# Latent attention in one TensorE kernel: value products in three rounded passes, two query tiles at a time

## The reference, cut to what matters

```python
def attend(q, k, v):
    s = jnp.einsum('bqhd,bkhd->bhqk', q, k).astype(jnp.float32) * (1.0 / math.sqrt(q.shape[-1]))
    p = jax.nn.softmax(s, axis=-1)
    return jnp.einsum('bhqk,bkhe->bqhe', p.astype(v.dtype), v)

def blocked_attention(q, k, v):          # q swept over 128-query blocks
    qb = q.reshape(B, L // Q_BLOCK, Q_BLOCK, H, d).swapaxes(0, 1)
    out = lax.map(lambda qi: attend(qi, k, v), qb)

y_mla = blocked_attention(q_m, jnp.concatenate([k_mc, k_m], axis=1), jnp.concatenate([mvc, mv], axis=1))
```

## Time and profile before

| | |
|---|---|
| median of 3 runs | 2731.52 us (2730.34 to 2733.38) |
| the profiled execution: its own time, its span | 2732.97 us, 2731.2 us |
| PE busy, share of the span | 2622.6 us, 96% |
| DVE busy, ACT busy, POOL busy | 1453.3 us, 1060.7 us, 484.9 us |
| mean granted clock of PE | 0.992 |
| the phase `mla`, first score to last value product | 481.7 to 684.1 us |

### The profile page before, as it was taken

The page is one execution under the profiler, slowest core; times in us unless marked ns, Lnnn a source line. Parts: engine busy times, 40 slices in busy tenths (PEclk is TensorE's granted clock), DMA queues, the critical chain, the costliest instruction groups (busy, mean ns, idle before and its releaser), DMA issues. The chain is left out here.

```text
span 2731.2 us, 36346 instructions
## 1 busy us (share of the span) xinstructions
PE 2622.6 (96%) x14641; PEld 2274.8 (83%) x14641; DVE 1453.3 (53%) x2039; ACT 1060.7 (39%) x1788; POOL 484.9 (18%) x323
## 2 busy tenths in 40 slices
PE   6999979999999999999999999999999999999999
PEld 2777777999777888888888999879989998878977
DVE  5745572433457666666658625447743524427751
ACT  3411543444245334334235224157732223237740
POOL 0001221332000000000000011048820002009930
PEclk9999999999999999999999999999999999999999
DMA  6543101000211121121121225332122113243222
GB/s 240 174 142 102 55 8 53 15 1 1 108 42 60 33 60 60 33 62 57 37 62 50 101 51 117 79 81 48 44 110 90 60 43 86 59 109 84 47 88 82
DMA packets 69683, 193.68 MB, mean 71 GB/s; under 512 B 8080, under 2 KB 26896, under 8 KB 68624
## 3 DMA queue, kind: packets, MB, share of 16 engines
q1 hardware_dynamic: 69520, 191.41, 23.2%
HBM read 148.88 MB, written 19.07 MB: 61 GB/s over the span
## 5 line engine op out<-in xcount | busy, mean ns | idle before, releaser
L2679 DVE SCALAR_TENSOR_TENSOR res<-ps,gates,res 128x1024 f32<-128x1024 f32 x120 | 148.6, 1279 | 100.0 <-PE ps L2804 100.0
L1319 PE MATMUL ps<-h_hi,pf_wh 128*128 128x346 f32 (+2 forms) x800 | 184.4, 334 | 0.2
L2538 ACT ACTIVATE wo_wh<-ff_raw 128x512 fp32r<-128x512 f32 x120 | 75.3, 628 | 278.7 <-DVE ff_raw L2649 114.2
L1319 PE MATMUL ps<-h_lo,pf_wh 128*128 128x346 f32 (+2 forms) x800 | 182.9, 332 | 0.0
L1948 DVE TENSOR_REDUCE da_negmax<-ps 128x1 f32<-128x1040 f32 x136 | 167.6, 1236 | 18.9 <-PE ps L1798 11.5
L1933 POOL TENSOR_TENSOR da_E<-da_E,da_F 128x1040 f32<-128x1040 f32 x68 | 164.7, 2422 | 5.7
L2804 PE MATMUL ps<-ff_h_hi,wo_wh 128*128 128x512 f32 x512 | 157.8, 389 | 1.4 <-DVE res L2679 1.3
L1841 PE MATMUL ps<-da_aT,v 128*128 128x128 f32 (+1 forms) x1224 | 157.5, 274 | 0.7 <-ACT qk L1905 0.7
L2804 PE MATMUL ps<-ff_h_lo,wo_wh 128*128 128x512 f32 x512 | 157.7, 389 | 0.0
L2804 PE MATMUL ps<-ff_h_hi,wo_wl 128*128 128x512 f32 x512 | 157.6, 389 | 0.0
L909 POOL MEMSET h_hi<- 128x112 f32 x2 | 0.4, 194 | 870.9 <-POOLq L66 870.9
(11 more groups left out here) (546 smaller groups left out, 6208.7 us busy)
## 6 DMA issues: line engine op xcount, KB each, us to landing
ff_raw<-w_ff SPq DMA_DIRECT2D x48, 512.0 KB, 3.5
ada_w<-w_ada SPq DMA_DIRECT2D x16, 1024.0 KB, 7.6
ff_raw<-w_in SPq DMA_DIRECT2D x20, 512.0 KB, 3.8
pf_raw<-w_in SPq DMA_DIRECT2D x20, 512.0 KB, 4.0
wo_raw<-w_out SPq DMA_DIRECT2D x18, 512.0 KB, 4.9
residual_spill<-res SPq DMA_DIRECT2D x16, 520.0 KB, 3.0
st_q<-st_q_rounded SPq DMA_DIRECT2D x32, 260.0 KB, 5.4
ada_w<-w_ada SPq DMA_DIRECT2D x4, 2048.0 KB, 17.0
```

Source lines behind the costliest of these rows:

```text
L1319: pe.matmul(bank(i * 2 + s, s)[c], wh[:, s, q * P:(q + 1) * P], x(q)[:, a:a + ln], start=(q == 0 and n == 0), stop=False)
L2538: act.activation(ring(wh, i), src, ACT.Copy).then_inc(s_hi, 1)
L2679: last = dve.scalar_tensor_tensor(out=res[:, m, :], in0=k.ps[:, b:b + 2, :].rearrange("p c w -> p (c w)"), scalar=gate[:, m:m + 1], in1=re ...
```

## The change

The value product is made in three rounded passes, and for two query tiles together.

- `mv` writes the values as `vh` (ACT) and `vl` (DVE).
- The turned E goes to `aT_hi` and `aT_lo`, each with room for the two tiles of a pair side by side (256 columns per key tile). There is one such pair of buffers, not two.
- ACT rounds batches 0 and 2 (`round_turned`). DVE makes both parts of batch 1 and the rests of batches 0 and 2 (`rest_turned`); the rest of batch 2 stands behind the reciprocal, the others ahead of it.
- `pv` runs only in turns with odd i, and does 30 float32r products of 256 columns. It waits for the rests of batches 0 and 1, and from key tile 8 on for that of batch 2.
- PE may write bank 6 again when DVE's rest is done (`s_lo`) and not when ACT's copy is; `out` copies 256 columns once per pair.

```diff
@@ turn (PE)
                         if g:
-                            pe.wait_ge(s_at, 2 * g)
+                            pe.wait_ge(s_lo, 3 * g)
                     elif b == 1:
-                        if g:
-                            pe.wait_ge(s_o, g)
+                        if g >= 2 and g % 2 == 0:
+                            pe.wait_ge(s_o, g // 2)
                     else:
-                        pe.wait_ge(s_at, 2 * g + 1)
+                        pe.wait_ge(s_lo, 3 * g + 1)
@@ pv (PE)
-                    pe.wait_ge(s_at1, g + 1)
-                    pe.wait_ge(s_at, 2 * g + 1)
+                    h = g // NQ
+                    pe.wait_ge(s_lo, 3 * g + 2)
                     for t in range(NT):
                         if t == 8:
-                            pe.wait_ge(s_at, 2 * g + 2)
-                        mm = pe.matmul(k.ps[:, 7, 0:P], v(g // NQ, t), aT[g % 2][:, t, :], start=(t == 0), stop=(t == NT - 1))
+                            pe.wait_ge(s_lo, 3 * g + 3)
+                        for n, (x, a) in enumerate(((v(0, h, t), aT_hi), (v(0, h, t), aT_lo), (v(1, h, t), aT_hi))):
+                            mm = pe.matmul(k.ps[:, 7, 0:2 * P], x, a[:, t].rearrange("p g q -> p (g q)"),
+                                           start=(t == 0 and n == 0), stop=(t == NT - 1 and n == 2))
@@ the loop (PE)
                         turn(i, 2)
-                        pv(i)
+                        if i % 2:
+                            pv(i)
@@ ACT
+                def round_turned(g, b):
+                    hi, _, src = turned(g, b)
+                    act.wait_ge(s_T, 3 * g + b + 1)
+                    if g >= 2 and b == 0:
+                        act.wait_ge(s_pv, g // 2)
+                    act.activation(hi, src, ACT.Copy).then_inc(s_hi, 1)
                 def out(g):
-                    act.wait_ge(s_pv, g + 1)
-                    act.activation(o_dst(g // NQ, (g % NQ) * P, P), k.ps[:, 7, 0:P], ACT.Copy).then_inc(s_o, 1)
+                    act.wait_ge(s_pv, g // 2 + 1)
+                    act.activation(o_dst(g // NQ, (g % NQ - 1) * P, 2 * P), k.ps[:, 7, 0:2 * P], ACT.Copy).then_inc(s_o, 1)
@@ DVE
+                def rest_turned(g, b):
+                    hi, lo, src = turned(g, b)
+                    if b == 1:
+                        dve.wait_ge(s_T, 3 * g + 2)
+                        dve.tensor_copy(hi, src).then_inc(s_hi1, 1)
+                        dve.wait_ge(s_hi1, g + 1)
+                    else:
+                        dve.wait_ge(s_hi, 2 * g + b // 2 + 1)
+                    dve.tensor_tensor(lo, src, hi.bitcast(F32), ALU.subtract).then_inc(s_lo, 1)
                     if i >= 0:
-                        evacuate(dve, i, 1, s_at1)
+                        rest_turned(i, 0)
+                        rest_turned(i, 1)
                     if 1 <= g <= NG:
                         ...                      # the reciprocal of tile g - 1
+                    if i >= 0:
+                        rest_turned(i, 2)
                     if g < NG:
                         ...                      # the maximum of tile g and its negative
@@ latent_attention
-                list(range(0, LT, P)), lambda t: (v[:, t, :],), preloaded=True, behind=4, then=...)
+                list(range(0, LT, P)), lambda t: (vh[:, t, :], vl[:, t, :]), preloaded=True, behind=4, then=...)
```

More of the change, by code:

```diff
@@ L2088, in latent_heads @@
         E = [k.sb(f"{name}_E{i}", [P, n_keys], e0 + i * (4 * n_keys + 32)) for i in range(3)]
-        aT = [k.sb(f"{name}_aT{i}", [P, NT, P], at0 + i * NT * 512) for i in range(2)]
+        aT_hi, aT_lo = (k.sb(f"{name}_aT_{n}", [P, NT, 2, P], at0 + i * NT * 1024, F32R) for i, n in enumerate(("hi", "lo")))
         mx = k.sb(f"{name}_max", [P, 4], k.small0)
@@ L2094, in latent_heads @@
         s_S, s_mx, s_nm, s_exp, s_rec, s_A = (k.sem(f"{name}_{n}") for n in ("scores", "max", "negmax", "exp", "rec", "A"))
-        s_T, s_at, s_at1, s_pv, s_o = (k.sem(f"{name}_{n}") for n in ("turned", "aT", "aT_middle", "pv", "o"))
+        s_T, s_hi, s_hi1, s_lo, s_pv, s_o = (k.sem(f"{name}_{n}") for n in ("turned", "aT_hi", "aT_hi_middle", "aT_lo", "pv", "o"))
         splits.open(s_S, NQ, 0)
@@ L2159, in _, with turned @@
                         turn(i, 2)
-                        pv(i)
[L2162 to L2166, removed]
+                        if i % 2:
+                            pv(i)
+            def turned(g, b):
                 nb = len(batch[b])
-                dst = aT[g % 2][:, 4 * b:4 * b + nb, :]
-                src = k.ps[:, bank[b], 0:nb * P].rearrange("p (t q) -> p t q", t=nb)
-                (eng.activation(dst, src, ACT.Copy) if sem is s_at else eng.tensor_copy(dst, src)).then_inc(sem, 1)
+                hi, lo = (x[:, 4 * b:4 * b + nb, g % 2, :] for x in (aT_hi, aT_lo))
+                return hi, lo, k.ps[:, bank[b], 0:nb * P].rearrange("p (t q) -> p t q", t=nb)
             @block.scalar
@@ L2192, in _ @@
                     i = g - LAG
-                    if i >= 1:
+                    if i >= 2 and i % 2 == 0:
                         out(i - 1)
                     if 0 <= i < NG:
-                        evacuate(act, i, 0, s_at)
+                        round_turned(i, 0)
                     if 1 <= g <= NG:
@@ L2199, in _ @@
                     if 0 <= i < NG:
-                        evacuate(act, i, 2, s_at)
+                        round_turned(i, 2)
                     if g < NG and g // NQ + 1 < heads and 1 <= g % NQ <= splits.ACT_STEPS:
@@ L2311, in latent_attention @@
     v0 = F0 + 6 * L * 4
-    v = k.sb("mla_v", [P, LT // P, MH * MV], v0)
+    vh, vl = (k.sb(f"mla_v_{n}", [P, LT // P, MH * MV], v0 + i * (LT // P) * MH * MV * 4, F32R) for i, n in enumerate(("hi", "lo")))
     h0 = v0 + 2 * (LT // P) * MH * MV * 4
@@ L2320, in latent_attention @@
                 lambda q, a: kh[:, q, a:a + P], lambda q, a: kl[:, q, a:a + P],
-                list(range(0, LT, P)), lambda t: (v[:, t, :],), preloaded=True, behind=4, then=("uq", rows(d["w_uq"]), 3 * P, 2))
+                list(range(0, LT, P)), lambda t: (vh[:, t, :], vl[:, t, :]), preloaded=True, behind=4, then=("uq", rows(d["w_uq"]), 3 * P, 2))
     qpe = k.sb("q_pe", [P, MH, L], k.res0 - 512)
@@ L2334, in latent_attention @@
     splits = LatentSplits(k, lambda h: y[:, h, :], lambda h: qpe[:, h, :], lambda h: kraw[:, h, :], keys.ks, q_at, k_at)
-    latent_heads(nc, k, "mla", MH, L // P, splits, LT, lambda h, t: v[:, t, h * MV:(h + 1) * MV], 1.0 / math.sqrt(NOPE + ROPE),
+    latent_heads(nc, k, "mla", MH, L // P, splits, LT, lambda r, h, t: (vh, vl)[r][:, t, h * MV:(h + 1) * MV], 1.0 / math.sqrt(NOPE + ROPE),
                  lambda h, a, w: y[:, h, a:a + w], k.ring0, at0, ("wo1", rows(d["w_out"]), KD * P, 2), k.res0 + 25088)
```

## The result

The changed kernel takes 2758.66 us (median of 4, 2756.43 to 2761.16) against 2732.45 of the kernel before on the same chip (4 runs, 2730.34 to 2734.87): a ratio of 1.0096, interval 1.0078 to 1.0113. It is slower by 26.2 us; 2752.4 was forecast.

A forecast was written before the change was run, and what follows sets the result against it. PE's sum of work was taken to bound the kernel, at 12.48 us per pair. Pairs 15.2, last pair 3.2, clock 2.3 and mv 0.2 add 20.9 us to 2731.52, giving 2752.4 us, range 2745 to 2761.

The forecast's parts named there:

- The waits: PE per pair: 0.35 us for the exponential, 0.49 for POOL's scaled E, 1.10 for DVE's rest before the value product.
- PE's sum: PE's work per pair without waits: 12.48 - 4.47 + 3.54 = 11.55 us, 0.93 less than before.
- the shift at such a border: At float32 to float32r borders the first product starts about 0.08 us early; taken as unchanged since their number stays.
- The last pair: Last two tiles, with no scores to lie beside: from 9.10 to 12.28 us, +3.2.
- The clock's term: Last pair: PE waits some 2.6 us in one piece, the clock falls during the value product: +2.3 us (0 to 3.5).
- The phase mv: In mv, nine of ten new subtractions lie beside products; the last ends after PE's `busy` products: +0.2 us.
- The sum: Whole kernel: 15.2 + 3.2 + 2.3 + 0.2 = +20.9 us, giving 2752.4 us.
- The faster one: Rival: in the pairs the value product shrinks and nothing waits, -14.7 us, 2716.8 us; chance 0.06.
- about the same: Rival: half the waits in the pairs vanish because DVE's operations overlap more, 2729 to 2737 us; chance 0.04.
- The clock among the pairs: Rival: short waits pull the clock down in every pair, some +22 us on top, 2775 us; chance 0.05.
- The weight loads: Rival: weight loads of 0.19 us hold the 256-column products, 5.7 us per pair, +35 us, 2787; chance 0.02.
- The page against the row: DVE's dependent rest behind its copy costs 0.72 us by the row, 0.605 by the skill, 3.5 less in all; row taken.

The follow-up runs named there:

- best_small_middle: Changed kernel with even-turn exponential and reciprocal first, ACT rounding batch 1, odd-tile batches of 4, 2, 4, unread products in the last pair: 2730.35 us, repeated 2729.95.
- rests_left_out: Changed kernel without subtractions of the turned E; the third product reads the rounded part again, still 30 products per pair: 2726.88 us, 0.9980 of before.
- rounded_not_paired: Changed kernel with the value product in every turn, as 30 float32r products of 128 columns: 2817.70 us, 1.0307 of before.
- pair_only_f32: Kernel before with pairing alone: ten float32 products of 256 columns in odd turns, no rounding, no rests: 2743.15 us, 1.0046 of before.
- exp_ahead_even: Changed kernel with, in even turns, ACT's exponential ahead of rounding batch 0 and DVE's reciprocal ahead of the rests: 2749.29 us, 1.0067 of before.
- middle_copy_first: Changed kernel with DVE's copy of batch 1 made ahead of the rest of batch 0: 2750.88 us, 1.0070 of before.
- act_rounds_middle: Changed kernel with ACT rounding batch 1 right behind batch 0, in place of DVE's copy: 2744.66 us, 1.0050 of before.
- clock_kept_fewer: Changed kernel with 23 unread products filling PE's waits in the last two turns: 2757.90 us, 1.0096 of before.

## Why the forecast was right, point by point

**The waits** (forecast 0.35, 0.49 and 1.10): right in place, cause and size, by the table above and by the kernels that take them away: 0.85 us for the first two, and 1.63 us that go with the rests, for the second and the third. The waits were the heart of it. That DVE idles 40% of the time (it is busy for 119.37 / 15 = 8.0 us per pair; the forecast took 8.6) protected nothing; its first rest can only start 1.3 us behind the turn's first transposes, and then it has three operations in a row to do.

**PE's sum** (forecast 11.55): the mis-sized term is the value product, 3.66 for 3.54. The spacing was right, but the first float32r product after float32 transposes and a wait takes 0.22. In the kernel without rests the scores show the same behind their wait, 1.87 for 1.75. The forecast let the shift at such a border cancel because the number of borders stays. It cancels only where PE does not wait: in `best_small_middle` the first product takes 0.20 too, but it starts 0.03 us behind the start of the last transpose (592.22 to 592.25), and not 0.11. Behind a wait that early start is lost. Fifteen pairs give 204.84 - 187.18 = +17.7 where +15.2 was forecast.

**The last pair** (forecast +3.2, and +2.3 for the clock): 12.46 us at a kept clock for 12.28, and 3.1 for the clock: together +6.45 for +5.5. The clock's term was a guess: twice the 1.5 us of the earlier trace rows are 3.0, and the forecast gives no reason for its 2.3. The low stretch lasted 10.2 us and met 27 of the 30 products; that behind the wait of 2.32 us in the earlier trace rows lasted 3.4 us (714.53 to 717.94).

**The phase mv** (forecast +0.2): from ACT's last rounding to the first rounding of the next phase 2.08 us (428.09 to 430.17), and 1.88 before (431.12 to 433.00). Right.

```profile
428.09 0.60 ACT L1404 ACTIVATE mla_v_hi<-ps 128x512 fp32r<-128x512 f32 x1 [0.17 <-PEq L1468]
...
430.17 0.94 ACT L1207 ACTIVATE uq_wh<-uq_raw 128x384 fp32r<-128x384 f32 x2 [1.48 <-PEq L66]
```

**The sum.** Forecast 20.9; these parts measure 24.1 + 0.2 = 24.3, and the medians differ by 26.2 (21 to 31 by the interval). The terms that missed were all too small, none too large, and some 2 us lie outside all of these parts, which the forecast did not have; so 2758.66 lies near the upper end of the range, 2745 to 2761.

**The rivals.** The faster one needed waits below 0.93 per pair; 1.94 were forecast and there. Its pair is that of `rests_left_out`, less its one wait. For "about the same" half the waits had to vanish, and none did. The clock among the pairs stayed at 1.00 over 204.84 us, with two waits of 0.5 and 1.1 in each pair, so in this kernel the short waits did not pull it down, and the swing of which the Trainium skill tells ("TensorE: Matmul & The Clock Gate", "A second HAM failure mode: psum-queue depth-cycling") does not show here. But `rounded_not_paired` shows a fall in one of fifteen pairs with waits no longer than these, so they are not safe in general. Nor does the longest wait of a last pair tell how long the clock stays low there: behind 2.5 us it was 3.4 us in `rests_left_out` and 6.8 in `pair_only_f32`, behind 2.4 us 10.2 in the changed kernel, and in `exp_ahead_even` and `middle_copy_first` 10.2 as well with no wait above 1.9 and 1.7. The weight loads do not hold the 256-column products: 0.118 apart.

**The page against the row.** DVE's dependent rest starts 0.71 behind the copy (570.90 to 571.61), the copy 0.61 behind the rest before it (570.29 to 570.90). The Trainium skill ("VectorE: DVE Perf Modes", "The DRAIN you can't avoid") says that a semaphore behind each operation costs nothing extra; here an operation that waits for the result of the one before it starts 0.10 later than one that does not, and the row that the forecast went by (0.72) was right.

**What stays open.** The other 2 to 3 us. In the two profiled executions the part ahead of the attention is 2.8 us shorter after the change and the part behind it 5.8 longer (2052.63 against 2046.81), although nothing but `mv` is edited there. Ahead of the attention the clock stood at 0.50 for 30.7 us before and for 23.9 us after. Behind it the largest single piece lies at one border of phases. Windows of before there, and then of after:

```profile
1996.00:2006.00 10.00, 8.52 (x73) 8.36 (x73) 0.38 (x2) 3.76 (x9) 2.92 (x3) 1.00 0.00 1
2006.00:2016.00 10.00, 10.00 (x67) 9.04 (x67) 3.10 (x9) 1.57 (x5) 1.48 (x3) 1.00 0.98 391
```

```profile
2020.00:2030.00 10.00, 8.52 (x59) 8.36 (x58) 0.38 (x2) 3.32 (x7) 4.22 (x5) 0.78 0.15 42
2030.00:2040.00 10.00, 10.00 (x53) 9.49 (x54) 1.99 (x7) 1.56 (x5) 0.15 (x1) 0.70 0.91 391
```

PE meets the same gap of 1.48 us in both (busy 8.52 of 10), and the clock stays at 1.00 in the one execution and falls in the other: (0.22 + 0.30) x 10 us = 5.2 us of the full clock are lost, nearly all of them in work. In the profiles of all thirteen runs, before and after included, PE has a wait of 1.5 us at this border: in four (before, `pair_only_f32`, `act_rounds_middle`, `best_small_middle`) the clock stays at 1.00, in three it is low for 3.4 us and in six, after among them, for 10.2. The same part took 2047.35 us and 2054.05 us in two profiled executions of one and the same kernel, `best_small_middle`. So some us of every total here depend on how long each fall of the clock lasts in an execution, not on the change. The 3.1 us of `clock_kept_fewer` can be followed in its profiled execution: against that of the changed kernel its stage is 3.1 us shorter, but the part ahead of it is 3.1 us longer (481.98 for 478.91), with the clock at 0.50 for 30.7 us there as in the kernel before. So there the clock elsewhere hid the gain; for the medians this is not shown, and how the 2 to 3 us divide between chance and the change stays open.

## What to carry to other kernels

Before an operation is moved out of every second turn, ask what it covered: a value product of 2.15 us hid the exponential, the scaling and the copies, and an engine that is idle 40% of the time still stops PE when three dependent operations stand between PE's two steps. Write the timetable from start-to-start distances, own results included; here it put each event up to the value product within 0.04 us. Then the same table shows the repair: give each wait its own edit (a rounding to the engine with room, the exponential ahead of it), and check that the two do not trade their waits.

## What the runs showed that I had not expected

- A float32r product of 128 columns costs 0.111 us, one of 256 costs 0.118: twice the columns for 6% more.
- The first float32r product behind float32 ones and a wait takes 0.10 more (0.22 for 0.118; the scores 1.87 for 1.75). Without the wait it takes 0.20, but starts 0.08 early.
- The wait for POOL in the last pair, 2.4 us by the view, in a stretch where PE had little to do, halved the clock for 10.2 us; waits of 0.5 and 1.1 in every 13.65 us never moved it. Yet in `rounded_not_paired` it fell twice with no wait above 0.9 by the view: the length of the longest wait does not tell.
- The same gap of 1.48 us at a border of two untouched phases left the clock at 1.00 in one execution and lowered it in another (about 5 us lost). Two executions of one kernel differ by 6.7 us behind the attention.
